# Two attention blocks, a Fourier block and a gated feed-forward on one core: the order of row tiles in the first weight chunk

## The reference, cut to what matters

```
for l in range(2):                      # first block
    proj = x @ w_in[l]                  # 512 x 1024 @ 1024 x 2912
    ya, yb, yc, ym = four attentions on parts of proj (ym on mem @ w_mem_kv[l])
    y = concat(ya*silu(ag), yb*silu(bg), yc*silu(cg), ym*silu(mg)) @ w_out[l]
    x = layer_norm(alpha * x + y, ln_gain[l], ln_bias[l])
for l in range(2):                      # second block
    p = rmsnorm(x, norm1[l]) @ w_in_2[l]
    y_f = fourier_mix(p[..., :512]); y_a = windowed_gqa(q, k, v from p)
    x = x + concat(rmsnorm(y_f), rmsnorm(y_a)) @ w_o[l]
    up = dwconv_centred(rmsnorm(x, norm2[l]) @ w_up[l])
    x = x + (silu(gate) * val) @ w_down[l]
```

## Time and profile before

| | us |
|---|---|
| median of 3 runs | 1783.13 |
| lowest, highest | 1782.92, 1788.38 |
| profiled execution | 1784.2 |
| its span | 1782.2 |
| PE busy in the span | 1706.6 |
| DVE, ACT, POOL busy | 780.1, 696.1, 677.9 |

### The profile page before, as it was taken

The page is one execution under the profiler, slowest core; times in us unless marked ns, Lnnn a source line. Parts: engine busy times, 40 slices in busy tenths (PEclk is TensorE's granted clock), DMA queues, the critical chain, the costliest instruction groups (busy, mean ns, idle before and its releaser), DMA issues.

```text
span 1782.2 us, 24207 instructions
## 1 busy us (share of the span) xinstructions
PE 1706.6 (96%) x8858; PEld 1340.8 (75%) x8858; DVE 780.1 (44%) x1496; ACT 696.1 (39%) x1144; POOL 677.9 (38%) x523
## 2 busy tenths in 40 slices
PE   6999999999999979989999999999998999999999
PEld 5776568787566857867888888878776888888887
DVE  7226564402646264664455115522565355403540
ACT  4444462524446152554433223333354344313431
POOL 3432215443221542425443344345252534434443
PEclk9999999999999988989999999999998999999999
DMA  7220103221110211212222222223121222232222
GB/s 253 106 72 26 70 25 119 95 95 72 38 59 25 83 48 48 72 49 71 95 94 87 100 96 94 91 82 111 49 72 48 94 95 94 71 110 103 94 76 89
DMA packets 24608, 145.90 MB, mean 82 GB/s; under 512 B 3152, under 2 KB 3536, under 8 KB 10704
## 3 DMA queue, kind: packets, MB, share of 16 engines
q1 hardware_dynamic: 21840, 138.01, 22.2%
q10 hardware_dynamic: 2688, 6.82, 1.0%
HBM read 142.72 MB, written 2.10 MB: 81 GB/s over the span
## 4 chain that ended last, share of the span: by engine, by line
PE 68%; issue 20%; POOL 7%; DVE 2%; ACT 2%; DMA 1%; POOLq 0%; ACTq 0%; DVEq 0%
PE ring L520 58%; POOL w_lo L506 7%; PE outs L580 2%; PE scores L566 1%; PE ring L566 1%; PE ring L604 1%; PE scores L590 1%; PE ring L660 1%; PE ring L590 1%; DMA xt<-in_x 1%; PE ring L922 1%; PE ring L634 1%; DVE g L1737 0%; ACT probs L1071 0%; ACT xh L1253 0%
## 5 line engine op out<-in xcount | busy, mean ns | idle before, releaser
L506 POOL TENSOR_TENSOR w_lo<-w_stage,w_hi 128x258 fp32r<-128x258 f32 (+5 forms) x471 | 644.3, 1400 | 1061.2 <-ACT w_hi L1026 660.5
L520 PE MATMUL ring<-xh,w_lo 128*128 128x512 f32 x1296 | 517.2, 399 | 24.6 <-DVE w_lo L1444 10.9
L520 PE MATMUL ring<-xh,w_hi 128*128 128x512 f32 x1296 | 511.7, 395 | 0.0
L520 PE MATMUL ring<-xl,w_hi 128*128 128x512 f32 x1296 | 510.6, 394 | 0.0
L520 PEld LDWEIGHTS ring<-xh,w_lo 128*128 128x128 f32 x1296 | 244.5, 189 | 86.5 <-DVE w_lo L1444 10.9
L520 PEld LDWEIGHTS ring<-xh,w_hi 128*128 128x128 f32 x1296 | 244.2, 188 | 55.3
L520 PEld LDWEIGHTS ring<-xl,w_hi 128*128 128x128 f32 x1296 | 244.7, 189 | 53.1
L1375 ACT ACTIVATE w_hi<-w_stage 128x2048 fp32r<-128x2048 f32 (+2 forms) x70 | 116.6, 1666 | 158.8 <-PE ring L520 158.8
L1385 ACT ACTIVATE g<-ring,convw 128x512 f32<-128x512 f32 x88 | 68.2, 779 | 245.3 <-DVE ring L1876 245.3
L1026 ACT ACTIVATE w_hi<-w_stage 128x2064 fp32r<-128x2064 f32 (+2 forms) x81 | 123.5, 1537 | 93.0 <-PE ring L520 92.5
L1858 DVE TENSOR_TENSOR xt<-xt,ring 128x512 f32<-128x512 f32 x48 | 33.0, 687 | 248.3 <-PE ring L520 248.3
(11 more groups left out here) (288 smaller groups left out, 2273.0 us busy)
## 6 DMA issues: line engine op xcount, KB each, us to landing
w_stage<-in_mixed SPq DMA_DIRECT2D x62, 1032.0 KB, 4.8
w_stage<-in_up SPq DMA_DIRECT2D x44, 1024.0 KB, 4.8
w_stage<-in_down SPq DMA_DIRECT2D x16, 768.0 KB, 4.3
w_stage<-in_down SPq DMA_DIRECT2D x16, 640.0 KB, 3.8
xt<-in_x ACTq DMA_DIRECT2D x4, 512.0 KB, 11.6
out_t<-xt ACTq DMA_DIRECT2D x8, 256.0 KB, 2.0
mem_f<-in_mem SPq DMA_DIRECT2D x1, 1024.0 KB, 9.8
bias_r<-in_relb SPq DMA_DIRECT2D x1, 1024.0 KB, 11.1
```

The costliest lines, as they stand in the source:

```text
L506: ins = nc.gpsimd.tensor_tensor(w_lo[:, slot, cols], source[:, cols], w_hi[:, slot, cols].bitcast(F32), ALU.subtract)
L520: ins = nc.tensor.matmul(o, lhs, rhs, start=start, stop=stop, skip_group_check=True)
```

## The change

Two functions are added on PE. `proj_both` acquires two banks and takes each row tile for both tiles of the chunk before it goes to the next row tile. It replaces `proj` for the first chunk of both layers of the first block and for the first query chunk of both layers of the second block. `out_projection` does the same in the first of four chunks and keeps the old order in the other three, but acquires both banks of each chunk at its start; it is written out in place of the loop, at four places. Nothing changes on the other engines.

```diff
--- before.py
+++ after.py
@@ -553,6 +553,32 @@
                         pe.wait_ge(S("x_split"), ready + k + 1)
                     r3(o[:, :], wtile(w_hi, slot, k, t), wtile(w_lo, slot, k, t), xh[:, k, :], xl[:, k, :],
                        k == 0, k == KD - 1, k == KD - 1)
+
+            def proj_both(names, slot, ready=None, halves=False):
+
+                o = [acquire(name) for name in names]
+                for k in range(KD):
+                    if halves and k == 0:
+                        pe.wait_ge(S("first_split"), 1)
+                    if halves and k == KD // 2:
+                        pe.wait_ge(S("w_split"), 1)
+                    if ready is not None:
+                        pe.wait_ge(S("x_split"), ready + k + 1)
+                    for t in range(2):
+                        r3(o[t][:, :], wtile(w_hi, slot, k, t), wtile(w_lo, slot, k, t), xh[:, k, :], xl[:, k, :],
+                           k == 0, k == KD - 1, k == KD - 1)
+
+            def out_projection(name, l, c, ready, xs, x_h, x_l):
+
+                for n in range(KD // 2):
+                    begin_chunk(c + n)
+                    o = [acquire((name, l, 2 * n + t)) for t in range(2)]
+                    steps = [(i, t) for i in range(KD) for t in range(2)] if n == 0 else [(i, t) for t in range(2) for i in range(KD)]
+                    for i, t in steps:
+                        if n == 0 and t == 0:
+                            pe.wait_ge(S("mix_split"), ready + i + 1)
+                        r3(o[t][:, :], wtile(w_hi, (c + n) % 2, xs[i], t), wtile(w_lo, (c + n) % 2, xs[i], t), x_h[:, xs[i], :], x_l[:, xs[i], :],
+                           i == 0, i == KD - 1, i == KD - 1)
 
             def attention(pairs, l, block, between):
 
@@ -847,8 +873,11 @@
                     c = b1_chunk(l, s)
                     if c > 0:
                         begin_chunk(c)
-                    for t in range(2):
-                        proj(("w", l, W_IN_TILES[2 * s + t]), c % 2, t, ready=KD * l if s + t == 0 else None, halves=c + t == 0)
+                    if s == 0:
+                        proj_both([("w", l, t) for t in W_IN_TILES[0:2]], c % 2, ready=KD * l, halves=c == 0)
+                    else:
+                        for t in range(2):
+                            proj(("w", l, W_IN_TILES[2 * s + t]), c % 2, t)
                     if l == 0:
                         for t in range(2):
                             memory(l, s, t)
@@ -864,18 +893,7 @@
                     transpose_all(("tv", l, f"av{t}"), ("w", l, f"av{t}"), qb[:, t, :])
                 attention(PAIRS[l], l, 1, later_projections(l, c0))
 
-                c = c0 + 13
-                with pe.Fori(0, 2) as i:
-                    for s in range(2):
-                        begin_chunk(i * 2 + (c + s))
-                        for t in range(2):
-                            o = acquire(("wout", l, 2 * s + t), i, 1)
-                            for n, k in enumerate(OUT_ORDER):
-                                if s + t == 0:
-                                    pe.wait_ge(S("mix_split"), KD * l + n + 1)
-                                r3(o[:, :], wtile(w_hi, (c + s) % 2, k, t), wtile(w_lo, (c + s) % 2, k, t), xh[:, k, :], xl[:, k, :],
-                                   n == 0, n == KD - 1, n == KD - 1)
-
+                out_projection("wout", l, c0 + 13, KD * l, OUT_ORDER, xh, xl)
 
                 ahead = l + 1 < DEPTH
                 if ahead:
@@ -894,13 +912,12 @@
 
             for l in range(DEPTH):
                 c0 = b2_chunk(l, 0)
-                for t in range(4):
-                    c = c0 + t // 2
-                    if t % 2 == 0:
-                        begin_chunk(c)
-                    proj(("q", l, t), c % 2, t % 2, ready=KD * (DEPTH + 2 * l) if t == 0 else None)
-                    if t == 1:
-                        mean(("ms", 2 * l), 0, [g[:, 0, :]], after("sq_sum", (KD - 1) * (2 * l + 1) - 1))
+                begin_chunk(c0)
+                proj_both([("q", l, t) for t in range(2)], c0 % 2, ready=KD * (DEPTH + 2 * l))
+                mean(("ms", 2 * l), 0, [g[:, 0, :]], after("sq_sum", (KD - 1) * (2 * l + 1) - 1))
+                begin_chunk(c0 + 1)
+                for t in range(2, 4):
+                    proj(("q", l, t), (c0 + 1) % 2, t % 2)
                     if t == 2:
                         pe.wait_ge(S("norm_inv"), 2 * l + 1)
                         spread(("inv_bc", 2 * l), rtok, 0)
@@ -948,18 +965,7 @@
                 pe.wait_ge(S("mix_inv"), l + 1)
                 spread(("yf_bc", l), rtok, 0)
                 spread(("ya_bc", l), rtok, 4)
-                c = c0 + 8
-                with pe.Fori(0, 2) as i:
-                    for s in range(2):
-                        begin_chunk(i * 2 + (c + s))
-                        for t in range(2):
-                            name = ("wo", l, 2 * s + t)
-                            o = acquire(name, i, 1)
-                            for k in range(KD):
-                                if s + t == 0:
-                                    pe.wait_ge(S("mix_split"), KD * (DEPTH + l) + k + 1)
-                                r3(o[:, :], wtile(w_hi, (c + s) % 2, k, t), wtile(w_lo, (c + s) % 2, k, t), mix_h[:, k, :], mix_l[:, k, :],
-                                   k == 0, k == KD - 1, k == KD - 1)
+                out_projection("wo", l, c0 + 8, KD * (DEPTH + l), range(KD), mix_h, mix_l)
 
                 c = c0 + 12
                 for h, (f0, nf) in enumerate(HALVES):
```

## The result

The changed kernel took **1791.78 us** (median of 16 runs, 1787.36 to 1798.51) against 1783.95 us for the kernel before (16 runs, 1776.91 to 1792.92): a ratio of 1.0040, interval 1.0025 to 1.0056. A second set gave 1791.46 us and 1.0029, interval 1.0011 to 1.0048. By the two ratios the change makes the kernel 5 to 7 us slower. The forecast was 1785.5 us, with 1781.0 to 1789.5 as its range: the sign of its sum (+2.4 us) was right, the size was not.

The account below looks back on a forecast made before the run. PE, busy 96% of the span, was taken as the bound. A +0.4, B 0, C -0.1 + 0.7, E +1.5 and F -0.1 summed to +2.4 us: 1785.5 us against the median, range 1781.0 to 1789.5.

Parts of the forecast that it names:

- A: Start of the kernel: pair ends 1.4 us sooner, memory projection still starts at 26.87 us; gain 0, clock loss 0.4 us.
- C: First chunk of layer 1, first block: gain 0.1 us, 2.5 us becomes a wait on POOL, clock loss 0.7 us.
- E: First query chunk, second block, layer 0: gain 0, wait before the mean grows to 5.0 us, clock loss 1.5 us.
- Rival 1: The waits at the start, layer 1, queries and output projections are simply gained: 7.9 us, so 1775.2 us; chance 0.05.
- B: Output projections of the first block, both layers: both banks acquired at each chunk's start, cost 0.
- F: Output projection of the second block, first layer: at most 0.1 us gained, late third-chunk rounding covered by 0.6 us.
- H: Output projection of the second block, second layer: nothing gained, cost 0.
- the prediction's own signs of being wrong: Mean much before 663 us, layer 1's chunk 2 before 351, or ring-bank or w_lo waits in the written-out projections.
- rival 3: Late weights: third chunk's rounding slips in the second block's output projections, 5.5 us on top, 1788.6 us; chance 0.05.
- The clock: Gathered idle time drops PE's clock: loses 0.4 us at the start, 0.7 in layer 1's first chunk, 1.5 at the queries.
- rival 2: The clock makes it slower behind the gathered waits at the queries, layer 1 and start: up to 1789.7 us; chance 0.08.

Follow-up runs that it names:

- the start only: New row-tile order in the very first chunk alone, all else as in the kernel before: ratio 0.9995, interval 0.998 to 1.001.
- the two parts alone: New order only in layer 1's first chunk (1.0035, again 1.0026), or only in the second block's first query chunks (1.0048, again 1.0043), against the kernel before.
- The filled kernels: New order with unread matmuls in its gathered waits, against the kernel before: first chunk of layer 1 alone 1.0005, query chunks alone 0.9979, whole change 0.9992.
- layer 1: New order in the first chunk of layer 1 of the first block alone, against the kernel before: ratio 1.0035, a second time 1.0026.

## Why the prediction was wrong

**Where the time would be swallowed** (A, C, E: gain 0 to 0.1) held. The memory projection starts at 27.00 us. Its wait is 1.98 us where 3.3 was forecast, because the first chunk ran at the lower clock until 16.70 us (before until 13.58) and so didn't end sooner; in the second profile and with the start only it is 2.67 and 2.64 us. Chunk 2 of layer 1 starts 0.06 us after POOL's end (349.26 + 4.56 = 353.82). The mean starts at 666.50 us against 663.10, a shift of 3.40 us that was there before the stage (+3.42): gain 0.0, and its wait is 5.04 us, where 5.0 was forecast (3.67 in the second profile, whose first row tiles were slow for longer). Rival 1 falls with this.

**Output projections** (B, F, H: cost 0, F gains 0.1). Held in time: the pair in F takes 819.98 - 805.92 = 14.06 us, before 14.01. In H one of the prediction's own signs of being wrong appeared, a wait on w_lo: the second chunk waits 0.24 us on POOL. It costs nothing, since the pair takes 13.83 us there against 14.07 before, and it isn't rival 3, which was about the third chunk; that one starts without a wait. By themselves these parts ran at 1.0008. Rival 3 is not what happened.

**The clock** is the step that failed, by size. It was priced for E at "1.5 us, between 0 and 2.3", for C at "half, 0.7 us, between 0 and 1.5", for A at 0.4. At the places the profiles show E 2.1 to 2.3 and C 1.4: both paid nearly their upper bounds, in four profiles out of four each, and not another value in each execution. The middle value for C was the mistake: it stood between one row that cost nothing and one that cost 1.5 us at nearly the same idle time, and the waits that came, 3.3 us in two profiles and 1.99 in two, cost 1.4 us each time. For E, the eight matmuls of the mean were left out of the count: they took 1.70 instead of 0.88 us before nine more matmuls at 0.43 us. The same step also rests on a lucky profile: the forecast read that the 1.3 us at 663.10 us cost no clock, but behind the same wait clock is lost in six of nine profiles.

A has a mistake of its own. It cost 0.64 us in the first profile, 0.00 in the second and 0.01 with the start only (the first row of the table, less the 0.12, 0.51 and 0.00 us by which ACT's rounding at 12.23 us was already late). "PE is the bound behind each of them, so a loss stays" doesn't hold there: with the memory projection at full pace PE waits 1.29 us for POOL's low part, so POOL ends the stage, and the slow stretch of the earlier trace rows cost the kernel before next to nothing.

That gives 4.2 and 3.6 us at the places in the two profiles, where the sum had +2.4. The rest of the 5 to 7 us is the second part of the error: the sum took every stretch without an edit as fixed, and they are not. Steps of -1.5, 0, +1.5 or +4.5 us at 751 to 790 us, and of 0, +1.6 or +3.0 us at 1314 to 1335, stand in profiles with the same matmuls there, and they lie in the clock. This is rival 2's side of the forecast (slower by the clock), which was given 0.08 and a threshold of all three places at full price; it didn't need that.

The Trainium skill, "TensorE: Matmul & The Clock Gate", Part 1, describes an oscillation: a PE that works in bursts with waits between them drops to the lower clock and has to earn the higher one again. The traces agree where a wait of 3.3 or 5.0 us stands between dense bursts (0.89 and 0.72 granted, 1.00 when filled), and show the same behind waits of 1.3 us in some executions.

**Still open:** why the two parts alone cost 4.6 to 8.6 us by their ratios when their places hold 1.4 and 2.2. The filled kernels show that the whole loss goes away with the wait, so it hangs on it, and by the estimate from the clocks of all runs 4.9 to 6.0 us of it are clock. But which later stage then goes slow differs between profiles of one kernel (layer 1), and the kernel with only the start changed shows the same later steps at no cost in its ratio. How the wait makes them more frequent wasn't found, nor what the up to 2.9 us of the queries beyond their clock are.

## What to carry to other kernels

Before small waits of PE are removed, look for what its next wait ends on: if that doesn't move, the small waits come back as one large one, and a large one can cost the clock that the small ones kept. Price that at its full value, one-column matmuls behind it included, and ask whether PE or another engine ends the stage behind it, since a slow stretch whose time PE would have waited out, as in stage A, costs next to nothing. Where a wait can't be removed, unread matmuls that fill it keep the clock; in this kernel a gain came only where the next wait was moved too, as with the weight chunk of the output projection. And one profile of the kernel before is one draw: read the granted clock of several runs before a stretch without slow matmuls is taken as safe.

## What the runs showed of the hardware that was not expected

- The length of a wait doesn't settle the clock behind it. 2.64 us of idle time at the start left the matmuls at full pace in one kernel, 1.89 us in the kernel before was followed by 16 matmuls at 1.2 GHz, and a wait of 1.99 us in stage C (the second profiles of layer 1 and of the kernel after) by eight. Behind the same wait of 1.24 to 1.28 us in the old stage E some eight matmuls are slow in six profiles and none in three.
- Stretches of one and the same code differ between profiles by a few fixed amounts (0, +1.6, +3.0 or -1.5, 0, +1.5, +4.5 us), not by a smooth spread, and the granted clock of the stretch gives the step (1.00, 0.96, 0.92 and 0.84 at 751 to 790 us).
- Among 124 runs of the kernel before, 0.01 of granted clock goes with 11.8 us, and most of their spread is that.
- Adding work can make this kernel faster: 13 unread matmuls, some 3 us of PE's time, in each of two places, together with a weight slot freed early, went with a gain of 4.8 and 6.4 us by the ratios.
